# A transformer's first stage: bias rows computed for 32 partitions, norm statistics finished in the first block, small values in mixer hooks

## The reference, cut to what matters

```python
for i in range(DEPTH):
    h = rms_norm(x, g_mix[i])                       # x * rsqrt(mean(x*x) + EPS) * g
    ... = jnp.split(h @ w_in[i], offsets, axis=-1)  # the mixer's dense projections
    lam = exp(sum(lambda_q1[i]*lambda_k1[i])) - exp(sum(lambda_q2[i]*lambda_k2[i])) + lam_init
    # differential attention, per block of 128 queries:
    bias = jnp.transpose(rel_bias[t5_bucket(kpos[None, :] - qpos[:, None])], (2, 0, 1))
    p1 = softmax(q1 @ k1 * scale + bias); p2 = softmax(q2 @ k2 * scale + bias)
    w = p1 - lam * p2
    o_d = spatial_gating(d_uv, g_sgu[i], w_spatial[i], b_spatial[i])
```

## Time and profile before

| | |
|---|---|
| median of three runs | 3655.0 us (3654.59 to 3658.4) |
| the profiled execution's own time | 3652.09 us |
| its span in the trace | 3650.3 us |
| TensorE busy | 3420.4 us, 94% of the span |
| first dense matmul of the mixer (L382) starts at | 44.24 us |

### The profile page before, as it was taken

How to read it: one execution, slowest core, us unless ns; L and a number is a source line. 1 busy time by engine, 2 the same in 40 slices (tenths; PEclk the granted TensorE clock), 3 DMA queues, 4 the chain that set the end, 5 groups by cost and what they waited for, 6 DMA issues and landing times. The chain is left out here.

```text
span 3650.3 us, 41915 instructions
## 1 busy us (share of the span) xinstructions
PE 3420.4 (94%) x17436; PEld 2449.3 (67%) x17436; DVE 1612.1 (44%) x2462; ACT 1138.2 (31%) x1765; POOL 79.8 (2%) x69
## 2 busy tenths in 40 slices
PE   7989998999989989998999988999999999989998
PEld 5767875444437767877444446876788888778887
DVE  3664542111125564552111114434656655466665
ACT  4553321010014454332101003444333344533333
POOL 0000000000000000000000000000000000000000
PEclk9999997999999999998999999999999999999999
DMA  5112254999982212235899992321222322122322
GB/s 168 53 44 79 65 182 189 409 409 409 409 335 95 76 45 67 73 110 209 352 409 409 409 409 100 105 82 47 81 93 94 103 73 78 58 70 93 104 93 70
DMA packets 324091, 616.69 MB, mean 169 GB/s; under 512 B 10864, under 2 KB 210288, under 8 KB 323904
## 3 DMA queue, kind: packets, MB, share of 16 engines
q1 hardware_dynamic: 323904, 614.01, 46.0%
HBM read 609.75 MB, written 4.23 MB: 168 GB/s over the span
## 5 line engine op out<-in xcount | busy, mean ns | idle before, releaser
L421 PE MATMUL bank<-h_hi,w_hi 128*128 128x512 f32 x1864 | 741.3, 398 | 11.1 <-DVE w_lo L207 10.0
L422 PE MATMUL bank<-h_lo,w_hi 128*128 128x512 f32 x1864 | 729.1, 391 | 0.0
L423 PE MATMUL bank<-h_hi,w_lo 128*128 128x512 f32 x1864 | 728.6, 391 | 0.0
L207 DVE TENSOR_TENSOR w_lo<-w_raw,w_hi 128x2048 fp32r<-128x2048 f32 (+1 forms) x209 | 424.1, 2029 | 224.9 <-ACT w_hi L199 224.4
L2063 PE MATMUL bank<-expert_w,gathered 128*64 128x512 f32 x2048 | 455.0, 599 | 30.6 <-DMA expert_w<-in_w_exp_up 27.2
L199 ACT ACTIVATE w_hi<-w_raw 128x2048 fp32r<-128x2048 f32 (+1 forms) x209 | 355.4, 1701 | 242.2 <-PE bank L423 203.8
L421 PEld LDWEIGHTS bank<-h_hi,w_hi 128*128 128x128 f32 x1864 | 351.5, 189 | 101.5 <-issue 16.5
L423 PEld LDWEIGHTS bank<-h_hi,w_lo 128*128 128x128 f32 x1864 | 351.3, 188 | 75.3
L422 PEld LDWEIGHTS bank<-h_lo,w_hi 128*128 128x128 f32 x1864 | 351.7, 189 | 73.0 <-issue 1.9
L2063 PEld LDWEIGHTS bank<-expert_w,gathered 128*64 128x64 f32 x2048 | 153.9, 138 | 314.7 <-issue 314.7
L2063 PE MATMUL bank<-expert_w,hidden_t 128*64 128x512 f32 x1024 | 228.5, 599 | 10.8 <-DMA expert_w<-in_w_exp_down 10.8
(11 more groups left out here) (411 smaller groups left out, 4599.8 us busy)
## 6 DMA issues: line engine op xcount, KB each, us to landing
expert_w<-in_w_exp_gate SPq DMA_DIRECT2D x64, 2048.0 KB, 23.9
expert_w<-in_w_exp_up SPq DMA_DIRECT2D x64, 2048.0 KB, 23.8
expert_w<-in_w_exp_down SPq DMA_DIRECT2D x64, 2048.0 KB, 23.9
w_raw<-in_ffn_w_up SPq DMA_DIRECT2D x44, 1024.0 KB, 5.1
w_raw<-in_w_branch_gate SPq DMA_DIRECT2D x64, 512.0 KB, 4.1
w_raw<-in_w_in SPq DMA_DIRECT2D x22, 1024.0 KB, 5.3
w_raw<-in_ffn_w_down SPq DMA_DIRECT2D x22, 1024.0 KB, 4.9
w_raw<-in_hgrn_w_in SPq DMA_DIRECT2D x16, 1024.0 KB, 5.3
```

Source lines behind the costliest of these rows:

```text
L207: dve.tensor_tensor(self.w_lo[n % 2][:, 0:e], self.raw[n % self.RAW][:, 0:e], self.w_hi[n % 2][:, 0:e].bitcast(F32), ALU.subtract).then_in ...
L421: pe.matmul(out, st[0], mv[0], start=(j == 0), stop=False)
L422: pe.matmul(out, st[0], mv[1], start=False, stop=False)
L423: last = pe.matmul(out, st[1], mv[0], start=False, stop=(j == len(g.steps) - 1))
```

## The change

- TensorE makes the bias rows of all four heads at once: the table now has 32 equal columns per head (32 x 128 in all), so that two matmuls leave head h's row in partitions 32h to 32h+31. ScalarE copies the two results out only in the mixer's `act_main`. The four stores, now in `side_loads`, read 32 partitions and write each row four times.
- The five loads that the norm and the bias rows need are issued by ScalarE; SyncE issues the first weight tile straight after `x`, then the other constants, then the second weight tile.
- All eight squares are made and added up in the first block, by VectorE (7 adds instead of 5), so TensorE sums one tile over the partitions instead of three. Sums, root and reciprocal are in the first block; only the spread stays in the second.
- The low half of the first weight tile is made in the second block. `cols` and `w_router` are loaded behind weight tile 2, and the small values are made in the hooks of tiles 2 to 4.

```diff
@@ class StartNorm(Norm)
+    def gather_squares(self, dve):
+        for kt in range(1, KT):
+            dve.wait_ge(*self.squared(kt + 1))
+            if kt >= 2:
+                dve.wait_ge(*self.gathered_to(kt - 1))
+            dve.tensor_tensor(self.sq[:, 0, :], self.sq[:, 0, :], self.sq[:, kt, :], ALU.add).then_inc(*self.gathered.inc())
+
+    def sums(self, pe):
+        pe.wait_ge(*self.gathered_to(KT - 1))
+        for tb in range(TB):
+            last = pe.matmul(self.bank[:, tb:tb + 1], self.sq[:, 0, tb * P:(tb + 1) * P], self.v.ones[:, 0:1], start=(tb == 0), stop=(tb == TB - 1))
+        last.then_inc(*self.summed.inc())
+
+    def act_start(self, act):
+        pass
+
+    def dve_start(self, dve):
+        pass
+
+    def pe_before_tile(self, pe):
+        self.spread_to(pe, self.bank, self.v.rstd)
+
+    def act_main(self, act):
+        v = self.v
+        super().act_main(act)
+        for i in range(2):
+            act.activation(v.rel_wide[:, i * S:(i + 1) * S], v.ps[3 + i][:], ACT.Copy).then_inc(*v.sig("rel_copied").inc())
@@ start_stage
-            sp.dma_start(v.gains[:], v.io["gains"]).then_inc(*gained.dma())
-            for dst, src in v.const_loads:
+            first, second = mixer_first(v)
+            v.ring.load(sp, 0, first)
+            for dst, src in v.const_loads[2:]:
                 sp.dma_start(dst, src).then_inc(*loaded.dma())
-            for n, srcs in enumerate(mixer_first(v)):
-                v.ring.load(sp, n, srcs)
-            sp.dma_start(onehot[:], v.io["c_onehot"]).then_inc(*tables.dma())
-            sp.dma_start(table[:], v.io["rel_rep"]).then_inc(*tables.dma())
-            small.load(sp)
-            for h in range(4):
-                sp.wait_ge(*copied.ge(2 * h + 2))
-                sp.dma_start(scratch[h:h + 1, :].rearrange("a (p w) -> p (a w)", w=W), wide[:, h, :]).then_inc(*v.rel_stored.dma())
-            sp.wait_ge(*loaded.ge(16 * len(v.const_loads)))
+            v.ring.load(sp, 1, second)
+            sp.wait_ge(*loaded.ge(16 * len(v.const_loads[2:])))
 
         @block.tensor
         def _(pe):
             pe.wait_ge(*tables.ge(32))
-            for i in range(8):
-                if i >= 4:
-
-                    pe.wait_ge(*copied.ge(i - 3))
-                pe.matmul(v.ps[i % 4][:], table[:, i // 2, :], onehot[:, (i % 2) * S:(i % 2 + 1) * S], start=True, stop=True).then_inc(*made.inc())
+            for i in range(2):
+                pe.matmul(v.ps[3 + i][:], table[:], onehot[:, i * S:(i + 1) * S], start=True, stop=True).then_inc(*made.inc())
+            pe.wait_ge(*early.ge(48))
+            norm.sums(pe)
 
         @block.scalar
         def _(act):
-            for kt in range(KT - 1):
+            for dst, src in ((table[:], v.io["rel_rep"]), (onehot[:], v.io["c_onehot"])):
+                act.dma_start(dst, src).then_inc(*tables.dma())
+            for dst, src in v.const_loads[0:2] + [(v.gains[:], v.io["gains"])]:
+                act.dma_start(dst, src).then_inc(*early.dma())
+            for kt in range(KT):
                 norm.square(act, kt)
+            act.wait_ge(*early.ge(48))
+            norm.root_table(act)
+            norm.root(act)
             v.ring.high(act, 0)
-            for i in range(8):
-                act.wait_ge(*made.ge(i + 1))
-                act.activation(wide[:, i // 2, (i % 2) * S:(i % 2 + 1) * S], v.ps[i % 4][:], ACT.Copy).then_inc(*copied.inc())
-            small.act(act)
-            act.wait_ge(*loaded.ge(16 * len(v.const_loads)))
-            norm.root_table(act)
...
             norm.gather_squares(dve)
-            v.ring.rest(dve, 0)
-            small.dve_sums(dve)
-            small.dve_lambda(dve)
+            norm.reciprocal(dve)
@@ mixer, side_loads
+        if n == 2 and v.layer.start == 0:
+            v.small_values.load(sp)
+            sp.wait_ge(*sig("rel_copied").ge(2))
+            for h in range(4):
+                dst = v.rel_scratch[h:h + 1, :].rearrange("a (p r w) -> (a p) r w", r=4, w=REL_W)
+                sp.dma_start(dst, v.rel_wide[32 * h:32 * h + 32, :].unsqueeze(1).to_broadcast([32, 4, REL_W])).then_inc(*v.rel_stored.dma())
...
+    if layer.start == 0:
+        v.small_values.wire(tiles)
```

More of the change, by code:

```diff
@@ L771, in start_stage @@
     W, K = REL_W, 1024
-    scratch = v.rel_scratch = nc.dram_tensor("rel_scratch", [4, P * W], F32, kind="Internal").ap()
+    v.rel_scratch = nc.dram_tensor("rel_scratch", [4, P * W], F32, kind="Internal").ap()
     def place(name, shape, at):
         return nc.alloc_sbuf_tensor_at(name, shape, F32, offset=v.layer_base + at)
-    wide, onehot, table = place("rel_wide", [P, 4, W], 84 * K), place("bucket_onehot", [32, W], 64 * K), place("rel_table", [32, 4, P], 68 * K)
-    tables, loaded, gained, made, copied = (sig(n) for n in ("rel_tables_loaded", "constants_loaded", "gains_loaded", "rel_made", "rel_copied"))
+    v.rel_wide, onehot, table = place("rel_wide", [P, W], 84 * K), place("bucket_onehot", [32, W], 64 * K), place("rel_table", [32, P], 68 * K)
+    tables, loaded, early, made = sig("rel_tables_loaded"), sig("constants_loaded"), sig("norm_constants_loaded"), sig("rel_made")
     gain_squares = sig("gain_squares")
-    small = v.small_values
     with nc.Block() as block:
@@ L824, in _ @@
             dve.memset(v.ones_row[:], 1.0)
-            dve.wait_ge(*gained.ge(16))
             order(dve.memset(v.ones_gain[:], 1.0))
+            norm.gather_squares(dve)
+            dve.wait_ge(*early.ge(48))
             dve.tensor_tensor(v.ones_gain[:, :, 1], v.gains[:, 48:56], v.gains[:, 48:56], ALU.mult)
             dve.tensor_tensor(v.gain_pair[:], v.gains[:, 48:56], v.gains[:, 64:72], ALU.mult).then_inc(*gain_squares.inc())
-            norm.gather_squares(dve)
-            v.ring.rest(dve, 0)
-            small.dve_sums(dve)
-            small.dve_lambda(dve)
+            norm.reciprocal(dve)
     sig.stage_end()
@@ L3084, in laid_out @@
     io["b_spatial_r"] = np.transpose(np.repeat(inp["b_spatial"].reshape(L, 2, 2, 1, P), 64, axis=3).reshape(L, 2, P, P), (0, 2, 1, 3))
-    io["rel_rep"] = np.repeat(inp["rel_bias"][:, :, None], P, axis=2)
+    io["rel_rep"] = np.repeat(inp["rel_bias"], 32, axis=1)
     io["w_forget"] = np.pad(inp["att_w_in_2"][0][:, 3072:3088], ((0, 0), (0, P - 16)))
```

## The result

The changed kernel took 3638.2 us (median of five runs, 3635.8 to 3639.5) where the kernel before took 3654.6 beside it: a ratio of 0.9955, with a 95% interval of 0.9941 to 0.9970. Between the two profiled executions, 3652.1 and 3635.8, lie 16.3 us, not the 24.0 of the sum. The time, 3638.25 before rounding, is 0.25 us past the upper end of the range.

What follows compares the result with a forecast made beforehand. TensorE, busy 3420.4 of 3650.3 us, was taken as the bound, full from the first dense matmul. Its 24.0 us advance gave 3652.1 - 24.0 = 3628.1 profiled, 3631 as median; range 3623 to 3638, own range 3626 to 3636.

Steps and rivals of the forecast that it cites:

- The mark: Start of the first dense matmul on TensorE: claimed to move from 44.24 to 20.2 us, 24.0 us earlier.
- chain B: Start, loads: second weight tile lands at 17.5, then its `w_hi` and h_hi; first dense matmul at 20.2 us.
- chain A: Start, norm: squares, adds, sums, root, `w_hi` 0, barrier, `w_lo` 0, scale; first dense matmul at 19.2 us.
- my estimate from it was 0.8 us by bytes: Start, DMA: five loads of 0.31 MB delay x by 0.8 us, putting the norm's chain at 20.0 us.
- ScalarE's loads and bias rows: First block: tables land near 5 to 6 us; two bias matmuls, 3.5 us on TensorE, hidden if tables land by 7.7.
- Rival 2: Start: ScalarE's tables land only at 18.02, first dense matmul at 29.5, 14.7 us won, 3640; chance 0.05.
- the same seven: First weight tile: seven dense matmuls at the lower clock, 0.444 us each, as before the change.
- rival 1: First weight tile: clock rises later, other 41 matmuls at the lower level cost 8.9 us, 3640; chance 0.07.
- The mixer's costs: Mixer: bias-row copies 1.2 us, later weight tiles, stores and small values all hidden; 3.6 us if small values' cover were gone.
- The repeated stores: Mixer, SyncE: four issues of about 0.5 us, landed at 30.5; a rival with 78 us each gave 3669, chance 0.02.
- The sum: Whole program: the first dense matmul's 24.0 us come off the end, 3652.1 to 3628.1 profiled, median 3631.
- The sign that the prediction had named: Profile after: forecast is wrong if the first dense matmul is past 22 us or the span falls by less than it.

Runs made afterwards that it cites:

- bias rows made four times: Changed kernel with its two bias matmuls made four times over, same operands and banks, nothing else put back: 3642.4 us, ratio 0.9953 to 0.9978.
- the dummies: Changed kernel plus unread bf16 matmuls in TensorE's idle time before the first weight tile: 27 of them 3628.8 us, 10 3628.4, 27 with only the tables on ScalarE's queue 3629.8.
- small values early: Changed kernel with the small values' loads, sums, exponentials and difference back in the first stage, none in the mixer: 3638.6 us, ratio 0.9940 to 0.9968.
- the two, four and eight fills: Changed kernel with two, four or eight extra fills of a small row on VectorE ahead of the first tile's scaling: 3632.7, 3635.2 and 3634.7 us.
- the loads behind x: Changed kernel with its five early loads issued by SyncE again, behind x and ahead of the first weight tile; two series: 3632.5 and 3633.5 us.
- the late statistics: Changed kernel with the eighth square, sums over three tiles, root and reciprocal back in the second block: 3635.8 us, ratio 0.9935 to 0.9963.

## Why the prediction missed

**The mark: 20.2 forecast, 21.43, 20.17, 21.39, 20.80 and 20.34 measured.** Near, and in part by luck: it was forecast from chain B, and chain A, forecast at 19.2, set it in all five profiles. Chain A was undersized by what the second queue does to x: "With eight squares the last one ends at 8.67 + 1.15 = 9.8" kept x's landings of before, and in the first profile the last one ended at 12.3. Everything after it was sized right: sums 1.84, then root and `w_hi` 0 (ready at 17.37), barrier 0.3, `w_lo` 2.3, and 1.54 from the scale to the matmul. The Trainium skill (DMA: Bandwidth & Descriptors, section Issuing engines are not separate DMA queues) had the direction: the loads share the same 16 DMA engines, and my estimate from it was 0.8 us by bytes. The profiles with and without ScalarE's loads show 0.9 to 2.3, on average 1.6, so they agree with the direction, and the share by bytes was too small; the pieces of x, 1.4 us apart on one queue, came 1.6 to 1.9 apart in the first profile, the first already 1.4 late. Chain B was right within 0.7: 18.18 instead of 17.5.

**ScalarE's loads and bias rows: right.** The one-hot table landed at 7.05, and the four bias instructions took 3.78, hidden behind the adds. Rival 2 did not occur.

**The clock at the first tile: "the same seven" was one draw of a number that scatters.** 14 matmuls ran at the lower level in the first profile, 10, 7, 7 and 12 in the other four; the two profiles of the kernel before have 7 and 9. The first tile ended 12.3 to 13.8 us after the mark in the five profiles, mean 13.0, against 12.4 and 12.8 before: 1.4 us in the first pair, 0.3 on average, which is within the scatter. In the first pair it is rival 1's mechanism at a sixth of its price. That the 14 us of bias matmuls didn't keep the clock up was right: bias rows made four times had 12 slow matmuls behind them, and the kernel before with 2 of its 8 had 13. The Trainium skill (TensorE: Matmul & The Clock Gate, Part 1, What's actually happening) says that activity releases the throttle; the dummies agree, and the 14 us of bias rows released nothing here.

**The mixer's costs: right, hidden as far as the runs show.** Rel_wide's copies at 25.80 for 1.07, the table load at 26.89, and ScalarE idle for 7.10 before 35.27. The repeated stores were worse than sized: issues of 0.6 to 2.4 us instead of 0.5, and a median of 7.3 us to landing instead of 2.6. First the timeline of SyncE's queue:

```profile
26.90 5.77 SPq L1780 DMA_DIRECT2D rel_scratch<-rel_wide  x4
```

and the list of DMA issues:

```profile
rel_scratch<-rel_wide SPq DMA_DIRECT2D x4, 512.0 KB, 7.3
```

They could afford it: the first reader came at 80.67, having waited for TensorE, not for them. The small values lie under idle time too, and there the experiment with small values early shows it. The timeline again, of ScalarE and VectorE:

```profile
62.16 0.19 ACT L766 ACTIVATE small<-small 128x1 f32<-128x1 f32 x1
...
80.67 0.69 DVE L1220 CUSTOM_DVE_ANT_0 probs<-bank,rel_bias 128x512 f32<-128x512 f32 x1 [1.43 <-PE bank L1208]
```

**The sum: the step that failed.** "What comes earlier with it comes off the end, as long as nothing behind it runs dry" is false by 5.1 us behind the first tile in the profiled pair and by about 4 on average (19.2 of 23.4, with 0.3 of it in the first tile). The sum had no term for the clock behind the first tile: it put it at nothing. Nothing ran dry; in the profiled pair the lost time is TensorE's own, at lower granted clock. The profiled pair fell 7.7 us short of the 24.0: 1.2 from the mark, 1.4 from the first tile, 5.1 from the later stretches. The sign that the prediction had named, a span that falls by less than the mark, came true: 16.3 against 22.8.

The second fault is the range. It allowed 1 to 4 us for scatter, from a single series of three. The medians of the changed kernel's five series differ by 6 us, and the first, on which the forecast is measured, was the slowest: 16.3 won where the average is 19.2. That this series fell 0.25 us outside the range and the other four inside is chance; the average, 3635.3, lies inside, 4.3 us above the forecast: 0.6 from the mark, 0.3 from the first tile, some 3.9 from the later stretches, less half a us because the kernel before averages 3654.5 and not 3655.0.

**What stays open.** Shown: in the profiled pair the loss is a few stretches of lower clock, it doesn't come from the small values' place, and the medians of the kernel before show none when its start is shifted by -7.5 or +3.0. Not shown: why the changed kernel meets it in four of five series (3613.5 to 3616.8 from the mark on, the second 3612.0) and the small values' kernel too, while the two, four and eight fills, the loads behind x and the late statistics lie at 3608.8 to 3612.1, bias rows four times between them at 3613.2, and the kernels with dummies at 3608.1 to 3609.0, some 2 us of it by their shorter first tile. Something in how the start leaves the machine could decide it. Chance in series of five, whose medians have a spread of about 2 us, can make part of the difference, though hardly all: by averages, the 30 runs of the fills, the loads behind x and the late statistics take 3610.7 from the mark on, as the kernel before does, and the 25 of the changed kernel 3614.5. These groups were put together after the results were known. I have no run that separates the causes.

## What to carry to other kernels

Where a program is bound by TensorE from a first matmul on, the mark is a good first sum but not the end. Here 4 of 23 us didn't arrive, and one series of three gave no measure of the scatter: repeat both kernels before sizing it, and don't read a few us off one pair of profiles. Loads that were put on a second queue to come early took time from the loads beside them, here about twice what their bytes say: price the delay of the others, and test whether moving only some of them helps (here it did not). Idle gaps of TensorE ahead of a dense stretch can be filled with matmuls that nobody reads; here the nine last ones did as much as all 27.

## What the runs showed of the hardware

- Five small loads of 0.31 MB on ScalarE's queue beside the 2 MB of x delayed the first use of x's last piece from 8.8 and 9.0 us (two profiles) to between 9.9 and 11.1 (five).
- Fourteen us of matmuls with 32 rows of float32 (0.88 us per instruction) left the clock at its lower level; nine bf16 matmuls of 128 rows, 4.1 us in all, around a spread of 2.05 us (and one more at 1.59) left it at the higher one.
- A store that reads 32 partitions four times (128 KB read, 512 KB written) landed after 7.3 us (median of four), where one that reads 128 partitions once took 2.6.
- Delaying the changed kernel's first dense matmul by 5 us did not make the program longer, and a first dense matmul 7.5 us earlier made the kernel before shorter by 7.4 (medians).
- The number of matmuls at the lower level at the start of the first tile differs between executions of one kernel: 14, 10, 7, 7 and 12 in five, and so do the stretches of low clock behind it, 202 to 236 us in all.
